# Value sums of the expert layer as 64x64 array quadrants, four accumulator banks, folded when the rows turn back

## The reference

```python
def block(xi):                       # 128 tokens, 2 blocks a layer
    q = (xi @ wq).reshape(Tb, 8, 2, 128)
    s = einsum('thcd,hcnd->thcn', q, subkeys)        # scores against 2 x 128 subkeys a head
    ...                                              # top 16 of each half, top 16 of their sums
    ue, ve = u[eidx], v[eidx]                        # 8 heads x 16 = 128 experts for each token
    act = gelu(einsum('td,thkd->thk', xi, ue))
    return einsum('thk,thkd->td', g * act, ve)       # the value sum
x = x + peer_ffn(rmsnorm(x, ffn_norm[l]), ...)
```

## Time and profile before

| | us |
|---|---|
| median of 3 runs (1931.65 to 1932.42) | 1931.69 |
| span of the profiled execution | 1928.8 |
| PE busy | 1591.4 |
| DVE busy | 1011.3 |
| ACT busy | 646.9 |
| gathers, share of the 16 DMA engines | 67.1% |

### The profile page before, as it was taken

One profiled execution on the slowest core, in us unless ns is written; L12 is line 12 of the kernel. 1 busy time (PEld: TensorE's weight loads), 2 busy tenths in 40 slices (PEclk: granted clock), 3 DMA queues, 4 the chain that ended last, 5 costly groups with the idle time before them and its releaser, 6 DMA issues.

```text
span 1928.8 us, 15560 instructions
## 1 busy us (share of the span) xinstructions
PE 1591.4 (83%) x4638; PEld 806.3 (42%) x4638; DVE 1011.3 (52%) x2487; ACT 646.9 (34%) x1897; POOL 514.9 (27%) x516
## 2 busy tenths in 40 slices
PE   7999989767877877787779989997788777877876
PEld 4777778222322222222237666763232222222222
DVE  3432238688544554445441632489874445444454
ACT  1243221423433333333332433123343333333333
POOL 0000001434433433333300000015444343333331
PEclk9999999999999999999989999999999999999999
DMA  8321224999999999999933222359999999999996
GB/s 304 131 88 44 101 108 184 390 416 421 422 421 422 421 422 422 421 421 422 421 154 131 88 104 93 118 221 422 421 421 421 422 421 421 422 421 422 421 421 287
DMA packets 107540, 610.20 MB, mean 316 GB/s; under 512 B 10032, under 2 KB 10176, under 8 KB 41280
## 3 DMA queue, kind: packets, MB, share of 16 engines
q0 software_dynamic: 73728, 536.90, 67.1%
q1 hardware_dynamic: 33728, 72.30, 10.3%
HBM read 608.12 MB, written 1.05 MB: 316 GB/s over the span
## 4 chain that ended last, share of the span: by engine, by line
DMA 45%; PE 38%; DVE 9%; ACT 5%; issue 2%; POOL 0%; SPq 0%; DVEq 0%; PEldq 0%; ACTq 0%
DMA arena<-in_experts,idxT 45%; PE psum L516 37%; DVE arena L1416 5%; ACT cst L882 1%; ACT gains L882 1%; ACT arena L882 1%; ACT gelus L882 1%; ACT L882 1%; DVE red L1385 1%; DVE kv L1377 0%; POOL arena L1710 0%; DMA vecs<-in_vecs 0%; ACT sqb L882 0%; DVE kv L1383 0%; DVE red L1200 0%
## 5 line engine op out<-in xcount | busy, mean ns | idle before, releaser
L516 PE MATMUL psum<-arena,cst 128*128 128x512 f32 (+2 forms) x2112 | 1029.4, 616 | 283.6 <-ACT cst L882 279.1
L1416 DVE CUSTOM_DVE_ANT_0 arena<-arena,xrow 128x1024 f32<-128x1024 f32 x512 | 624.4, 1224 | 537.7 <-DMA arena<-in_experts,idxT 537.0
L1710 POOL DMA_INDIRECT arena<-in_experts,idxT x512 | 514.7, 1005 | 1387.8 <-PE psum L516 790.0
L516 PEld LDWEIGHTS psum<-arena,cst 128*128 128x128 f32 x2112 | 367.1, 191 | 942.5 <-ACT cst L882 645.7
L882 ACT ACTIVATE gelus<-red 128x1 f32<-128x1 f32 x512 | 103.6, 202 | 770.2 <-DVE red L1416 769.9
L516 PE MATMUL psum<-hT,ring 128*128 128x256 f32 x1280 | 293.3, 390 | 6.1 <-DVE hT L1215 6.1
L516 PEld LDWEIGHTS psum<-hT,ring 128*128 128x128 f32 x1280 | 248.9, 196 | 47.5 <-issue 9.8
L882 ACT ACTIVATE cst<-cst,gains 128x128 f32<-128x128 f32 x512 | 206.2, 403 | 23.2 <-PE psum L516 6.7
L882 ACT ACTIVATE gains<-gelus,gateT 128x1 f32<-128x1 f32 x512 | 150.8, 294 | 17.0 <-ACT gelus L882 0.2
L882 ACT ACTIVATE arena<-psum 128x512 f32<-128x512 f32 (+3 forms) x89 | 47.8, 545 | 304.3 <-PE psum L516 304.0
L516 PE MATMUL psum<-mixT,ring 128*128 128x256 f32 x256 | 57.4, 387 | 2.5 <-DVE mixT L1689 2.5
(11 more groups left out here) (161 smaller groups left out, 672.1 us busy)
## 6 DMA issues: line engine op xcount, KB each, us to landing
ring<-in_peer_wq SPq DMA_DIRECT2D x8, 2048.0 KB, 8.1
ring<-in_ev_w_in SPq DMA_DIRECT2D x6, 2048.0 KB, 11.8
ring<-in_od_w_in SPq DMA_DIRECT2D x5, 2048.0 KB, 33.0
ring<-in_xa_wkv SPq DMA_DIRECT2D x4, 2048.0 KB, 7.9
arena<-in_experts,idxT POOLq DMA_INDIRECT x512, 15.3
ring<-in_ev_w_out SPq DMA_DIRECT2D x2, 2048.0 KB, 7.8
ring<-in_xa_wq SPq DMA_DIRECT2D x2, 2048.0 KB, 9.2
ring<-in_xa_wo SPq DMA_DIRECT2D x2, 2048.0 KB, 7.7
```

The costliest lines, as they stand in the source:

```text
L516: return nc.tensor.matmul(out, lhsT, rhs, start=start, stop=stop)
L1416: V.tensor_tensor_reduce(out=ut, in0=ut, in1=xrow[:, u // PAIRS, :], scale=1.0, scalar=0.0, op0=ALU.mult, op1=ALU.add, accum_out=dots[:, k ...
L1710: nc.gpsimd.indirect_dma_start(slot[slot_of(u)], None, d["experts"], bass.IndirectOffsetOnAxis(ap=idxT[:, u:u + 1], axis=0))\
```

## The change

The 128 x 128 diagonal has nothing but zeros in two of its four 64 x 64 blocks. The changed kernel multiplies the other two alone: rows 0 to 63 of v with the upper diagonal block, rows 64 to 127 with the lower one, each as a matmul of 64 rows by 64 columns, for two banks of 512 columns: four matmuls a unit instead of two. In even units the results go to the partitions they come from (straight), in odd units to the other half (crossed). The results of upper and lower rows go to different banks, so there are four accumulator banks. Each of them holds in one half of its partitions the sum of the even units and in the other half the sum of the odd ones. They are signalled full together behind the last unit. ACT copies four banks into a `yrow` twice as wide, and turning back is now 16 ordinary matmuls with a 128 x 64 constant `fold`, which has a one where the partition and the column agree modulo 64: it turns a block and adds its two halves in one step. There are two semaphores for taken units, one for each half of the rows, and POOL and ACT wait for both.

```diff
-        jobs.extend(f"acc{l}.{t}.{b}" for t in range(TT) for b in range(2))
+        jobs.extend(f"acc{l}.{t}.{b}" for t in range(TT) for b in range(4))
...
+    put("fold", p[:, 0:1] % 64 == np.arange(64)[None, :])
...
-        yrow = kv[:, 0:D]
+        yrow = kv[:].rearrange("p (r n) -> p r n", n=D)
...
-            eng.wait_ge(expert_mm, l * UNITS + u + 1)
+            for r in range(2):
+                eng.wait_ge(expert_mm[r], l * UNITS + u + 1)
...
-                    copied(pe, f"acc{l}.{t}.0", f"acc{l}.{t}.1")
+                    copied(pe, *parts(f"acc{l}.{t}.", 4))
                     for b in range(2):
                         o, done = job(f"back{l}.{t}.{b}")
                         for c in range(4):
-                            last = nc.tensor.transpose(o[:, c * P:(c + 1) * P],
-                                                       yrow[:, (4 * b + c) * P:(4 * b + c + 1) * P], ident)
+                            for r in range(2):
+                                at = c * P + 64 * r
+                                last = mm(o[:, at:at + 64], yrow[:, r, (4 * b + c) * P:(4 * b + c + 1) * P], const("fold"))
                         last.then_inc(done, 1)
...
-                        first = mm(o0, diag[:, u % DIAGS, :], v[:, 0:BANK], k == 0, k == PAIRS - 1)
-                        last = mm(o1, diag[:, u % DIAGS, :], v[:, BANK:D], k == 0, k == PAIRS - 1)
-                        if k == PAIRS - 1:
-                            first.then_inc(done0, 1)
-                        last.then_inc(expert_mm, 1)
+                        for b in range(2):
+                            for r in range(2):
+                                rows_in = slice(64 * r, 64 * r + 64)
+                                col = 64 * ((r + k) % 2)
+                                o, done = acc[2 * r + b]
+                                last = mm(o[col:col + 64], diag[rows_in, u % DIAGS, rows_in],
+                                          v[rows_in, b * BANK:(b + 1) * BANK], k < 2, k >= PAIRS - 2)
+                                if b == 1:
+                                    last.then_inc(expert_mm[r], 1)
...
-                    pe.wait_ge(expert_mm, l * UNITS + (t + 1) * PAIRS)
-                    pe.sem_inc(done1, 1)
+                    for r in range(2):
+                        pe.wait_ge(expert_mm[r], l * UNITS + (t + 1) * PAIRS)
+                    for o, done in acc:
+                        pe.sem_inc(done, 1)
...
-                    for b in range(2):
+                    for b in range(4):
                         o = full(act, f"acc{l}.{t}.{b}")
-                        fn(yrow[:, b * BANK:(b + 1) * BANK], o, ACT.Copy).then_inc(bank_free(f"acc{l}.{t}.{b}"), 1)
+                        fn(yrow[:, b // 2, b % 2 * BANK:(b % 2 + 1) * BANK], o, ACT.Copy)\
+                            .then_inc(bank_free(f"acc{l}.{t}.{b}"), 1)
```

More of the change, by code:

```diff
@@ L59 @@
 for _name, _n in (("ident", P), ("ones", P), ("head_ones", P), ("rot", P), ("tri", P),
-                  ("past", 3 * P), ("causal", 3 * P), ("iota", PE_K), ("inv_freq", 1),
+                  ("past", 3 * P), ("causal", 3 * P), ("iota", PE_K), ("inv_freq", 1), ("fold", P // 2),
                   ("levels", 8 * P)):
@@ L405, in trunk @@
         weighed = sem("weighed")
-        expert_mm = sem("expert_mm")
+        expert_mm = [sem(f"expert_mm{r}") for r in range(2)]
         stored = sem("stored")
@@ L662, in back @@
                         for c in range(4):
-                            last = nc.tensor.transpose(o[:, c * P:(c + 1) * P],
-                                                       yrow[:, (4 * b + c) * P:(4 * b + c + 1) * P], ident)
+                            for r in range(2):
+                                at = c * P + 64 * r
+                                last = mm(o[:, at:at + 64], yrow[:, r, (4 * b + c) * P:(4 * b + c + 1) * P], const("fold"))
                         last.then_inc(done, 1)
                 for t in range(TT):
-                    (o0, done0), (o1, done1) = job(f"acc{l}.{t}.0"), job(f"acc{l}.{t}.1")
+                    acc = [job(f"acc{l}.{t}.{b}") for b in range(4)]
                     for k in range(PAIRS):
```

## The result

The changed kernel takes 1944.92 us (median of 4 runs, 1940.65 to 1947.53), the kernel before 1932.06 beside it (4 runs): ratio 1.0063, 95% interval 1.0048 to 1.0077. It is slower by some 0.6%, 12.9 us. Predicted were 1941.5 us, and a range that holds the measured time.

The account below looks back on a forecast made before the run. Transfers, not PE, were taken to bound the kernel. The terms, 2 x (1.4 + 2.5) + 1.5 + 0.7 + 0.1 - 0.3 = +9.8 us, gave 1928.8 + 9.8 + 2.9 = 1941.5 us, range 1935.5 to 1948.

Parts of the forecast that it names:

- The unit is hidden: Expert units: the halves overlap, eight passes take 1.98 us, under the 2.48 us spacing set by transfers; no change.
- A: Expert units: the quadrants don't overlap, 3.44 us a unit, PE becomes the bound, about 2420 us; 8%.
- B: Gather slots: round latency limits and PE's part shortens; narrower weight load alone -3.5 us, or 1924 us in all; 5%.
- C: Expert units: slot latency limits and the unit lengthens to 2.4 us; +27, about 1969 us; 3%.
- Copies at the stage end: Each layer's end: four banks signalled together and copied behind the last pass, so turning starts later, +1.4 us.
- Turning: Each layer's end: 32 passes instead of eight transposes, 3.7 us, second add +2.5 us later; lower end +0.8.
- rival D: Layer ends: shorter tail, 64-column passes at half price, no low clock, better burst; +3.4, 1935 us; 9%.
- The clock: Turning at the layer ends: some passes run at the 1.2 GHz level, 1.5 us for both layers together.
- Run low already; that stays: Layer 1's first projections: already at the low clock in the kernel before, so no change.
- Instruction fetch: Whole program: near 4,900 more instructions, 0.3 MB at 422 GB/s, 0.7 us in a stage limited by transfers.
- Constants: Ahead of the first sum: 64 more constant columns, 32 KB, load before the vectors that release it, 0.1 us.
- burst: First units: PE works off gathers landed during the projections; overlapping crossed and straight quadrants shrink idle DMA time, -0.3.

Follow-up runs that it names:

- longer_unit: The kernel before with one more matmul of 256 columns in every unit, both banks signalled behind the last unit: 1935.34 us, ratio 1.0023.
- two_waits: The kernel before with a semaphore for each of a unit's two matmuls, both waited for, banks signalled together: 1931.89 us, one run.
- straight4: The changed kernel with straight quadrants only, four banks, and the eight transposes of before for turning back: 1937.23 us, ratio 1.0029.
- straight2: As straight4, but both halves of the rows in the same two banks, so two copies: 1933.27 us, ratio 1.0011.
- one_quadrant: As straight4, but all four matmuls of a unit in the upper left quadrant: 4152.72 us, one run.
- after_again: The changed kernel once more, unchanged, for a second trace: 1944.03 us, ratio 1.0065.
- before_warm_all: The kernel before with unused filler matmuls in every PE gap of 1.5 to 5.2 us around the stage changes: 1921.09 us, ratio 0.9947.
- after_warm_all: The changed kernel with all fillers of before_warm_all and two unused matmuls ahead of the turn: 1930.35 us, ratio 0.9993.
- before_warm: The kernel before with five unused matmuls in the idle time ahead of the normalization of layer 0's result: 1931.59 us, ratio 1.0.

## Why the prediction was right, point by point

- **The unit is hidden, and stays 2 us long.** Right: 1.93 us for eight passes (1.98 forecast), spacing 2.48, DMA share 1.01, and longer_unit shows that even 0.43 us more would have been hidden. Rivals A, B and C fall with it (B's first sum should read 64 x 0.05 = 3.2 us, not 3.5). The Trainium skill ("TensorE: Matmul & The Clock Gate", Part 3: Packing small matmuls) has matmuls start and end strictly in program order; by that the unit would have taken 2.41 us. The measured 1.93 decides against it, for these shapes.
- **Semaphores and waits, zero.** Right in time (two_waits, 1931.89 us). That POOL's issues grow from 1.0 to 1.66 us on the mean I had not seen coming: they now start beside the dot product on DVE. Each is still done 0.5 us before the next one starts.
- **Mid-stage turn, zero.** Right: both stages are as long as before, to 0.4 us.
- **Copies at the stage end, +1.4 a layer.** Nearly: straight4 puts them at 1.7. 0.5 of it is the common signal (straight2, two_waits), 1.2 the two more copies, for which I had reckoned 0.92.
- **Turning, +2.5 a layer at full clock.** Right: 3.76 us for 32 passes (3.7 forecast), and 11.21 - 8.78 = 2.4 between the changed kernel and straight4. The pace is that of full passes with 128 columns, 31 x 0.112 + 0.28, as reckoned from the weight loads; rival D's half price is out.
- **The clock, +1.5 for both layers.** The mechanism and its place were right, the size too small: 2.8 us in layer 0 and none in layer 1 in the profiled execution, 3.2 and 1.0 in the second one. I had also put layer 1's projections some 4 us late; with the turn's 2.8 us they start 6.2 us later than before. What I had no term for is that the projections themselves take 2.9 us more in some executions. "Run low already; that stays" held in the first execution (253.02 us against 253.00) and not in the second; straight2 and longer_unit show that it is no cost of the long tail alone.
- **Instruction fetch, +0.7.** Wrong. The queues did move 1.29 MB instead of 1.00 (4,804 more instructions, near the 4,900 forecast), but no stage became longer. The 0.3 MB at 422 GB/s was a sum made without asking when they are fetched.
- **Constants +0.1, burst -0.3.** Both too small to be told. The burst shows something else than I expected: in the first value sums of layer 1 the even and the odd unit do run side by side, with four weight loads every 0.43 us in the timeline. Two units then take 1.72 us instead of 3.44:

```profile
1298.38 0.24 PEld L518 LDWEIGHTS psum<-arena,cst 64*64 64x64 f32 x4 [0.19 <-issue]
1298.81 0.24 PEld L518 LDWEIGHTS psum<-arena,cst 64*64 64x64 f32 x4 [0.19 <-issue]
```

The straight quadrants of straight2 and straight4 have two loads in each 0.43 us there. This is what crossed and straight quadrants can give over straight ones, and it brings nothing here: PE finishes the burst sooner and then waits for ACT's diagonals and the transfers. Layer 1's stage is 0.3 us shorter, within what executions differ by.

In the first trace the two tails came out 1.9 us above their terms (11.2 for 9.3: +0.6 copies, +1.3 clock, the turning within 0.2 of its term), and everything else 1.6 below (-1.1 for +0.5, which were instructions, constants and burst). So 10.1 us of span stand against 9.8 forecast: the mechanism was right and the tail's sizes near, but that the sum meets the span to 0.3 us is luck. The median's difference, 12.9 us, is 3.1 above the forecast; in the second trace the clock's part is larger by about as much (+1.4 in the turns, +2.8 in the projections). The range held it, though its lower bound, 2 x (1.4 + 1.2), takes a 1.2 for the turning that the text works out nowhere (its lower end there is 0.8).

## What to carry to other kernels

Ask of a faster inner step first which resource holds the loop: here the transfers did, at a share of 1.01, so a PE unit that could have been twice as dense was worth nothing, and what it needed at the loop's end (more banks to copy, a fold for the transposes) was paid in full. Work behind the last unit should be priced at the clock that it will meet: where the clock fell behind a gap of 2.5 us, the 32 passes took nearly twice as long. If short gaps let the clock fall where PE does set the pace, fill all of them: one alone moved nothing, all together took 1931.99 to 1921.09 us.

## What the runs showed of the hardware

- The granted clock does not follow PE's busy share in the trace. One 64x64 quadrant at work for 200 of 200 us was granted 0.50 (one_quadrant); two at a time, at 155 to 156 of 200 us, were granted 1.00 (straight2 and the changed kernel). The folding passes with 64 moving columns filled 998 to 1000 of the changed kernel, and the granted clock there was 0.50 as well.
- The Trainium skill ("TensorEngine Tiling (Array Packing)", Gotcha 1: PSUM Pressure) says that different row tiles cannot access one PSUM bank at the same time. In straight2 the two halves write different partitions of one bank, and a unit takes the same 1.93 us; for this case the measurement decides.
- An indirect gather's issue keeps POOL busy for 0.94 us where it starts ahead of a dot product on DVE (606.55 against 606.98, before), and for 1.96 to 1.98 us where it starts just behind the start of one (two_waits, the changed kernel). It cost no time here, at a DMA share of 1.01.
- How long the clock stays low behind a fall differs between executions of one kernel, 17.1 and 20.5 us here. The projections of layer 1 take 2.8 to 3.0 us more where it returns 12.9 to 13.1 us behind the second add (after_again, straight2, longer_unit) than where it returns after 10.4 us. The runs agree better where the gaps are filled: 1.6 us from the lowest to the highest of 5 in before_warm_all, 3.8 of 10 in after_warm_all, 6.1 of 12 in before_warm, which fills one.
